# Scan stage of a hybrid block: order of VectorE's work across two steps

## The reference, cut to what matters

```python
def step(s, inp):                      # _gla_scan
    qc, kc, vc, gc = inp
    cum = jnp.cumsum(gc.astype(jnp.float32), axis=1)
    inter = jnp.einsum("blhk,bhkv->blhv", qc * jnp.exp(cum), s)
    ...
    s_new = s * jnp.exp(tot)[..., None] + jnp.einsum(
        "blhk,blhv->bhkv", kc * jnp.exp(tot[:, None] - cum), vc)

def step(s, inp):                      # _ssd_scan
    ...
    inter = jnp.einsum("bihn,bhpn->bihp", cc, s) * jnp.exp(cum)[..., None]
    w = (jnp.exp(tot[:, None] - cum) * dtc)[..., None]
    s_new = s * jnp.exp(tot)[:, :, None, None] + jnp.einsum("blhn,blhp->bhpn", bc * w, xc)
```

## Time and profile before

| | |
|---|---|
| median of 3 runs | 2765.26 us (2758.18 to 2767.77) |
| the profiled execution | 2763.02 us, its span 2761.3 us |
| busy in the span | TensorE 2573.4 us, VectorE 1601.2, ScalarE 1284.1, GpSimd 179.4 |
| the scan stage | about 306 to 448 us from the span's start |
| in it | TensorE busy 115.19 us, VectorE 107.25, ScalarE 57.33 of 142 |
| data moved in it | 0.46 MB |

### The profile page before, as it was taken

How to read it: one execution, slowest core, us unless ns; L and a number is a source line. 1 busy time by engine, 2 the same in 40 slices (tenths; PEclk the granted TensorE clock), 3 DMA queues, 4 the chain that set the end, 5 groups by cost and what they waited for, 6 DMA issues and landing times.

```text
span 2761.3 us, 31556 instructions
## 1 busy us (share of the span) xinstructions
PE 2573.4 (93%) x11516; PEld 1887.0 (68%) x11516; DVE 1601.2 (58%) x2329; ACT 1284.1 (47%) x1885; POOL 179.4 (6%) x201
## 2 busy tenths in 40 slices
PE   6899888999999999999998999979989999899997
PEld 2587666588878667578876666646766887766664
DVE  6636477322223458544456888854765344688885
ACT  5424544422222453543234788724444333288882
POOL 0000000000000001000001222100100000122210
PEclk9899999999999999999998999999999999999999
DMA  9511100222113222022134999851202122499992
GB/s 342 180 61 62 35 1 1 91 92 92 61 61 102 81 83 71 21 92 92 61 117 144 364 353 355 311 190 61 92 31 92 62 92 79 141 318 368 367 352 112
DMA packets 198221, 392.38 MB, mean 142 GB/s; under 512 B 24127, under 2 KB 54863, under 8 KB 198095
## 3 DMA queue, kind: packets, MB, share of 16 engines
q1 hardware_dynamic: 170912, 340.55, 35.2%
q10 hardware_dynamic: 14831, 33.38, 3.2%
q0 software_dynamic: 12352, 16.81, 1.9%
HBM read 386.48 MB, written 29.36 MB: 151 GB/s over the span
## 4 chain that ended last, share of the span: by engine, by line
PE 80%; DVE 8%; ACT 4%; DMA 3%; DVEq 2%; issue 2%; ACTq 1%; SPq 0%; POOL 0%; PEld 0%; POOLq 0%; PEldq 0%
PE banks L206 60%; PE banks L176 8%; PE banks L3048 2%; PE banks L182 2%; DMA ring<-in_w_exp_up 1%; DMA ring<-in_w_mod 1%; DVE arena L2229 1%; DVE ring_parts L485 1%; DVEq L2230 1%; PE banks L2051 1%; PE banks L2327 1%; PE banks L2702 1%; PE banks L1930 1%; PE banks L2035 1%; PE banks L2314 1%
## 5 line engine op out<-in xcount | busy, mean ns | idle before, releaser
L206 PE MATMUL banks<-hT_parts 128*128 128x512 f32 (+1 forms) x1376 | 545.2, 396 | 0.0
L206 PE MATMUL banks<-arena_parts,hT_parts 128*128 128x512 f32 (+1 forms) x1408 | 525.8, 396 | 7.5 <-DVEq L167 5.0
L206 PE MATMUL banks<-ring_parts,arena_parts 128*80 128x512 f32 (+2 forms) x1296 | 517.1, 399 | 0.0
L206 PE MATMUL banks<-hT_parts,arena_parts 128*128 128x512 f32 (+1 forms) x1248 | 453.7, 404 | 25.9 <-DVE ring_parts L236 8.2
L206 PE MATMUL banks<-arena_parts,ring_parts 128*128 128x512 f32 (+1 forms) x1168 | 454.6, 389 | 0.0
L206 PE MATMUL banks<-arena_parts 128*128 128x512 f32 (+3 forms) x1280 | 409.9, 391 | 10.3 <-DVEq L167 8.9
L236 DVE TENSOR_TENSOR ring_parts<-ring,hT_parts 128x1024 fp32r<-128x1024 f32 x148 | 181.3, 1225 | 327.4 <-ACT hT_parts L232 324.3
L232 ACT ACTIVATE hT_parts<-ring 128x1024 fp32r<-128x1024 f32 x148 | 156.6, 1058 | 377.3 <-PE banks L206 377.1
L3273 DVE TENSOR_TENSOR ring_parts<-ring,hT_parts 128x2048 fp32r<-128x2048 f32 x128 | 292.9, 2290 | 54.2 <-ACT hT_parts L3170 53.7
L206 PEld LDWEIGHTS banks<-arena_parts,hT_parts 128*128 128x128 f32 x1408 | 261.7, 188 | 69.3 <-DVEq L167 8.3
L206 PEld LDWEIGHTS banks<-hT_parts 128*128 128x128 f32 (+1 forms) x1376 | 239.4, 174 | 81.8 <-issue 1.6
(11 more groups left out here) (503 smaller groups left out, 3212.8 us busy)
## 6 DMA issues: line engine op xcount, KB each, us to landing
ring<-in_w_exp_gate SPq DMA_DIRECT2D x64, 1024.0 KB
ring<-in_w_exp_up SPq DMA_DIRECT2D x64, 1024.0 KB
ring<-in_w_exp_down SPq DMA_DIRECT2D x128, 512.0 KB
ring<-in_w_in SPq DMA_DIRECT2D x58, 1024.0 KB
ring<-in_w_mod SPq DMA_DIRECT2D x24, 1024.0 KB
ring<-in_w_gate SPq DMA_DIRECT2D x11, 1024.0 KB
ring<-in_w_up SPq DMA_DIRECT2D x11, 1024.0 KB
ring<-in_w_down SPq DMA_DIRECT2D x22, 512.0 KB
```

The source lines that it names most:

```text
L206: last = nc.tensor.matmul(out, l, r, start=start and i == 0, stop=stop and i == len(products) - 1)
```

## The change

The subtraction for `g_dist` and the small difference become `distances(n)`, and `g_q`, `g_k` with their drain become `decayed(n)`. Both are called for step 0 ahead of the loop. In the loop `distances(n + 1)` stands between the state-space output of step n and the wait for `ssd_bx`; `decayed(n + 1)` stands behind the update of `s_st` in a latent step (ahead of the output's copy) and behind `next_state()` in a context step. The number and the kinds of the instructions stay; TensorE's and ScalarE's programs stay too.

```diff
+            def distances(n):
+                s_sm = s_sm2[:, n % 2, :]
+                dve.wait_ge(S("gla_half"), n + 1)
+                V.tensor_tensor(g_dist, ps[:, 0, 0:256], g_half, ALU.subtract).then_inc(S("gla_dist"), 1)
+                dve.wait_ge(S("ssd_small"), n + 1)
+                V.tensor_tensor(s_sm[:, 24:32], s_sm[:, 8:16], s_sm[:, 0:8], ALU.subtract).then_inc(S("ssd_wd"), 1)
+
+            def decayed(n):
+                i = SCAN[n][1]
+                dve.wait_ge(S("gla_exp"), n + 1)
+                if i < LT:
+                    V.scalar_tensor_tensor(g_q, qk[:, i, 0:256], GK ** -0.5, g_eq, ALU.mult, ALU.mult)
+                V.tensor_tensor(g_k, qk[:, i, 256:512], g_ek, ALU.mult)
+                dve.drain().then_inc(S("gla_qk"), 1)
+
+            distances(0)
+            decayed(0)
             for n, (d, i) in enumerate(SCAN):
                 lat = i < LT
                 m += lat
+                ahead = n + 1 < len(SCAN)
...
-                dve.wait_ge(S("gla_half"), n + 1)
-                V.tensor_tensor(g_dist, ps[:, 0, 0:256], g_half, ALU.subtract).then_inc(S("gla_dist"), 1)
                 for j in range(2):
                     V.tensor_scalar(g_sd[:, j, :], g_s[:, j, :], g_ecol[:, j:j + 1], None, ALU.mult)
-
-                dve.wait_ge(S("ssd_small"), n + 1)
-                V.tensor_tensor(s_sm[:, 24:32], s_sm[:, 8:16], s_sm[:, 0:8], ALU.subtract).then_inc(S("ssd_wd"), 1)
-                dve.wait_ge(S("gla_exp"), n + 1)
-                if lat:
-                    V.scalar_tensor_tensor(g_q, qk[:, i, 0:256], GK ** -0.5, g_eq, ALU.mult, ALU.mult)
-                V.tensor_tensor(g_k, qk[:, i, 256:512], g_ek, ALU.mult)
-                dve.drain().then_inc(S("gla_qk"), 1)
 
                 dve.wait_ge(S("ssd_wexp"), n + 1)
...
+                if ahead:
+                    distances(n + 1)
                 dve.wait_ge(S("ssd_bx"), n + 1)
...
                 dve.drain().then_inc(S("ssd_state"), 1)
+                if lat and ahead:
+                    decayed(n + 1)
 
                 if lat:
                     dve.wait_ge(S("gla_out"), m)
...
                 else:
                     next_state()
+                    if ahead:
+                        decayed(n + 1)
```

## The result

Over 15 runs each, the changed kernel took 2775.42 us (2762.51 to 2780.15) and the kernel before 2765.68 us (2758.18 to 2769.94). The ratio is 1.0032, 95% interval 1.0022 to 1.0042: slower by 0.32%, some 9 us (the medians lie 9.7 apart). The profiled execution took 2777.14 us, its span 2775.4, which is 14.1 more than the one before.

A forecast was written before the change was run, and what follows sets the result against it. TensorE is busy for 93% of the span, but the change lies in the scan stage, where waits count. Waits of +5.7 and clock of +2.4 make +8.1 us, 2773.4 from the 2765.3 median; range 2765 to 2781.

The forecast's parts named there:

- (a): Forward latent-to-latent steps, n = 2, 3, 4: two VectorE waits go, mostly returning as waits for ScalarE; -0.4 us in all.
- (b): Backward latent-to-latent steps, n = 8, 9, 10: the wait in front of `g_q` becomes a plain gain; -1.1 us in all.
- (c): Latent to context, n = 5 to 6: `ssd_bx`'s product starts earlier; -0.8 us.
- (f): Start, n = 0: memsets and L1085 now stand between `g_k` and L1096; +0.6 us.
- (d): Context to context, n = 0 to 1 and 6 to 7: updates queue behind the distance's wait; +1.5 and +1.2 us.
- (e): Context to latent, n = 1 to 2 and 7 to 8: L1096 comes later; +2.5 and +2.2 us.
- ScalarE's S: End of ScalarE's last small column for the next step; in context steps `g_k` was to start 3.56 us later.
- (g): Latent steps n = 2 and 8 begin at TensorE's low clock behind 3.2 us gaps; +1.2 us twice, +2.4.
- The clock that holds: Rival: TensorE's clock does not fall behind the gaps, leaving +5.7 us, 2771.0; chance 0.22.
- The slower case: Rival: low clock lasts into the products with `s_w` at n = 2 and 8; +13.5 us, 2778.8; chance 0.2.
- No loss at all: Rival: VectorE does not hold up the context steps; -1.7 us, 2763.6; chance 0.05.
- the large gain: Rival: earlier keys also remove the 1.0 us wait in front of L1116, 7.8 us over 8 steps; chance 0.03.

The follow-up runs named there:

- held clock: Changed kernel and kernel before, each with products nobody reads placed in TensorE's gaps so its clock stays at full level: stage 141.4 and 136.0 us.
- the run with the states first: Changed kernel with the two states set to zero ahead of the first distance: stage 148.1 us, 6.56 us to the first `ssd_bx`.

## Why the prediction was right, step by step

The forecast was +8.1 us, 2773.4, on the border of what can be told; measured were 2775.42 and +0.32%, just beyond it, and the stage itself gave +7.9. The other 1.8 us of the medians' 9.7 are not located. The case with the greatest chance, the forecast, came in; of its two halves the runs give the sizes: the waits +5.7 forecast, 5.4 at a held clock; the clock +2.4 forecast, 2.6 (8.5 less 5.9).

(a) and (b), latent steps: -0.7 and -1.2, for -0.4 and -1.1. In (a) two spacings were too long: with no wait in front of it the copy hands over after 0.61 us and not 0.70, and the small difference takes 0.08 and not 0.10. The new wait for ScalarE at the distance is there, 0.23 us in each forward step.

(c), -0.8: the number is exact. Most of it was the low level that the old order's keys had there, since the old order reaches 7.60 at a held clock and the new one 7.48. (f), +0.6 for +0.7; the run with the states first gives it back.

(d) and (e), the context's waits. At a held clock the two orders differ by +1.5 in both loops (8.84 for 7.34, 8.84 for 7.35), forecast +1.5 and +1.2; into the latent steps by +1.5 and +1.9 (14.45 for 12.94, 14.81 for 12.95), forecast +2.5 and +2.2. These two were too large. Also at a held clock the way to the first `ssd_bx` differs by 1.1 and not by 0.6, and that to n = 6 by -0.1 and not -0.8, for the reason given at (c). The sum was right to 0.3 us with terms up to 1 us off on both sides; that these cancelled was luck. What was right is the chain from ScalarE's S on: for n = 7 it puts the key product at S + 4.06 and `ssd_bx`'s at S + 5.93, and in the changed kernel S was 391.11 and the two started at 395.15 and 397.02.

(g), the clock. The mechanism was right and its place was not. I put it all into the latent steps n = 2 and n = 8, at +1.2 each, with turns and products at twice their time; at n = 8 the turns and the key product were at full level. VectorE's wait of 2.5 us over 2 at L1119 shows it there, and the output followed L1104 by 7.15 us in both, where it had followed by 6.27 and 6.26: +0.9 each. But the low level also sat in the sums of n = 7 (1.06 us, 0.59 in a latent step), in front of ScalarE's S, which the new order put on the path: the loop of n = 6 to 7 took 11.8 us for 10.2 by (d), and the backward waits at the distance were 5.0 and 5.3 us and not 3 to 4. In the forward direction it was the other way: the sums ran at full level and the loop was 0.6 us below (d). The 2.6 us of both directions is therefore a figure of these executions and not of the two programs: one program's stage moved by 3.5 us between two executions (136.6 and 140.1), another's by 0.1 (140.2 and 140.3). That it met the +2.4 is luck in part.

The rivals. The clock that holds (+5.7) is refused by the granted clock of 0.52. The slower case, low level into the products with `s_w`, did not happen: they took 2.81 us in n = 8. No loss at all is refused by the waits at the distance, 17.7 us in the four steps behind a context step, and the large gain by L1124's wait, 7.8 us as before. The chances were near even between slower and same, and the result lay 0.02% beyond the border.

## What to carry to other kernels

Before work for the next step is pulled ahead, compare the time at which its inputs arrive with the end of the idle time that it is to fill: here the distance's inputs came 1.7 to 2.8 us after the result that the old wait was for, so it pushed 3.4 us of ready work behind itself. The same call moved by one place, behind the update of `s_st`, cost nothing in the context's steps and left the latent steps' gain of 1.8 us standing. And where an engine waits for another in short gaps, a delay of the other can cost a second time through TensorE's clock; measure with the clock held before dividing a loss among its causes.

## What the hardware showed that was not expected

The cost of the low level of TensorE's clock was not a constant of the program: with one and the same kernel the stage took 136.6 us in one execution and 140.1 in another, with the difference only in parts with or behind gaps of TensorE. And the kernel with work in it that nobody reads was 0.42% faster as a whole (ratio 0.9958, 11.3 us between the medians). Of that, 5.9 us are seen in the stage, in one profile of each; where the rest lies is not shown. The work was fifty products in six gaps of the old order, and it took the granted clock from 0.72 to 1.00 in the backward context steps.
